# Attention head by head, or in groups of heads that fill a bank of 512 columns

## What is computed

```python
# mixer_a, layers 0 and 3: 16 heads of 64; tokens see chunks of 64 up to their own
s = einsum('bqhd,bkhd->bhqk', qc, kb) * scale + bias          # bias: a table by distance
p = softmax(where(valid, s, NEG_INF)); o = einsum('bhqk,bkhd->bqhd', p, vb)
# mixer_c, layer 2: 8 heads x 2 maps, bias -slope*|distance|
a = p[:, 0] - lam_full * p[:, 1];      o = einsum('bhqk,bkhe->bqhe', a, v)   # e = 128
# second model, twice each:
# nsa_attention: 8 heads, three branches (7 or 15 compressed keys, selected, window), sum by gates
# mla_attention: 4 heads, logits (qn.kn + qp.kp) * scale, causal
# memory_cross_attention: 4 heads of 128 over 256 memory tokens
```

## Time and profile before

| | |
|---|---|
| median of 3 runs | 3524.96 us |
| profiled execution | 3519.57 us, span 3517.8 us |
| TensorE busy | 3267.9 us (93%), 22679 matmul records |
| VectorE busy | 1888.6 us (54%) |
| ScalarE busy | 1490.2 us (42%) |
| GpSimd busy | 71.9 us (2%) |
| granted TensorE clock, mean | 0.948 of 2.4 GHz |
| DMA | 533.95 MB, mean 152 GB/s |

### The profile page before, as it was taken

How to read it: one execution, slowest core, us unless ns; L and a number is a source line. 1 busy time by engine, 2 the same in 40 slices (tenths; PEclk the granted TensorE clock), 3 DMA queues, 4 the chain that set the end, 5 groups by cost and what they waited for, 6 DMA issues and landing times.

```text
span 3517.8 us, 53612 instructions
## 1 busy us (share of the span) xinstructions
PE 3267.9 (93%) x22679; PEld 3041.3 (86%) x22679; DVE 1888.6 (54%) x2615; ACT 1490.2 (42%) x2303; POOL 71.9 (2%) x146
## 2 busy tenths in 40 slices
PE   8998999999999996999999999988789999888899
PEld 8987998988989895998988998986689999767897
DVE  5555555546545466545555554665555447555554
ACT  4444444444444443444444444334344443344443
POOL 0000000000000000000000000000000000000000
PEclk9999999999999998999998999986899998779999
DMA  6552555555555551454563456440235565213354
GB/s 222 193 186 83 163 188 165 182 178 162 185 169 191 182 173 37 163 192 161 189 200 97 138 181 190 150 145 13 96 125 166 189 180 162 86 40 104 126 176 143
DMA packets 434402, 533.95 MB, mean 152 GB/s; under 512 B 27330, under 2 KB 398452, under 8 KB 434164
## 3 DMA queue, kind: packets, MB, share of 16 engines
q1 hardware_dynamic: 421220, 512.22, 44.8%
q10 hardware_dynamic: 12944, 18.31, 1.7%
HBM read 528.33 MB, written 1.11 MB: 151 GB/s over the span
## 4 chain that ended last, share of the span: by engine, by line
PE 85%; DVE 7%; ACT 4%; issue 2%; DMA 1%; POOL 1%; SPq 1%; ACTq 0%; DVEq 0%; POOLq 0%
PE bank L633 84%; ACT sb_prT L1031 1%; DVE sb_sc L1559 1%; DVE sb_nmax L1561 1%; PE bank L794 1%; DVE sb_hT_low L1514 1%; DMA sb_slot<-in_w_in_dram 1%; POOL sb_rstd L1353 1%; ACT sb_prT L993 1%; DVE sb_low L1435 1%; ACT sb_pr L1094 0%; ACT sb_high L1020 0%; PE bank L671 0%; ACT sb_hT_high L993 0%; DVE sb_oT_low L1516 0%
## 5 line engine op out<-in xcount | busy, mean ns | idle before, releaser
L1435 DVE TENSOR_TENSOR sb_low<-sb_slot,sb_high 128x2048 fp32r<-128x2048 f32 (+1 forms) x480 | 1094.3, 2283 | 712.0 <-ACT sb_high L1020 711.4
L633 PE MATMUL bank<-sb_hT_high,sb_high 128*128 128x256 f32 x4264 | 1214.5, 285 | 22.1 <-DVE sb_hT_low L1514 16.3
L633 PE MATMUL bank<-sb_hT_low,sb_high 128*128 128x256 f32 x4264 | 1210.2, 284 | 0.0
L633 PE MATMUL bank<-sb_hT_high,sb_low 128*128 128x256 f32 x4264 | 1209.8, 284 | 0.0
L1020 ACT ACTIVATE sb_high<-sb_slot 128x2048 fp32r<-128x2048 f32 (+1 forms) x480 | 912.1, 1905 | 676.6 <-PE bank L633 589.9
L633 PEld LDWEIGHTS bank<-sb_hT_high,sb_high 128*128 128x128 f32 x4264 | 823.0, 193 | 26.6 <-DVE sb_hT_low L1514 17.5
L633 PEld LDWEIGHTS bank<-sb_hT_low,sb_high 128*128 128x128 f32 x4264 | 823.0, 193 | 0.0
L633 PEld LDWEIGHTS bank<-sb_hT_high,sb_low 128*128 128x128 f32 x4264 | 822.2, 193 | 0.0
L1071 ACT ACTIVATE sb_prT<-bank 128x256 f32<-128x256 f32 x220 | 84.3, 383 | 699.2 <-PE bank L633 699.2
L633 PE MATMUL bank<-sb_low,sb_hidden_high 128*128 128x512 f32 x880 | 350.8, 399 | 0.0
L633 PE MATMUL bank<-sb_high,sb_hidden_high 128*128 128x512 f32 x880 | 346.7, 394 | 0.0
(11 more groups left out here) (209 smaller groups left out, 3464.5 us busy)
## 6 DMA issues: line engine op xcount, KB each, us to landing
sb_slot<-in_ff_w_in_dram SPq DMA_DIRECT2D x176, 1024.0 KB, 5.2
sb_slot<-in_ff_w_out_dram SPq DMA_DIRECT2D x88, 1024.0 KB, 5.0
sb_slot<-in_w_gate_up_dram SPq DMA_DIRECT2D x44, 1024.0 KB, 5.2
sb_slot<-in_w_in_dram SPq DMA_DIRECT2D x42, 1024.0 KB, 5.3
sb_slot<-in_a_w_qkv_dram SPq DMA_DIRECT2D x24, 1024.0 KB, 5.2
sb_slot<-in_w_down_dram SPq DMA_DIRECT2D x22, 1024.0 KB, 5.0
sb_slot<-in_c_w_qkv_dram SPq DMA_DIRECT2D x12, 1024.0 KB, 5.2
sb_slot<-in_a_w_o_dram SPq DMA_DIRECT2D x8, 1024.0 KB, 5.2
```

Of the source, the lines that this page charges most:

```text
L633: return nc.tensor.matmul(o, lhsT, rhs, start=start, stop=stop)
L1435: V.tensor_tensor(low[i][:, 0:size], slots[n % SLOTS][:, 0:size], high[i][:, 0:size].bitcast(F32), ALU.subtract) \
```

## The change

The heads of a stage are taken in groups: four where a head has at most 128 keys, two where it has 256, so that the scores of a group, and its turned blocks, fill at most one bank of 512 columns. `groups_of` makes the groups out of the units; each turn of the three engines is now a group.

- VectorE does one scale-and-bias operation for the group with a three-dimensional bias operand (heads x keys, reversed; for causal and cross stages one line repeated for each head; for the differential stage one operation for each pair of maps, so two at four heads), and one maximum that gives one column for each head.
- ScalarE does one exponential for each head as before, but writes it over the scores in `sc`; `pr` is gone.
- One copy moves the turned blocks of the whole group. ScalarE does it for groups of 256 keys and now ahead of the exponentials of group i; VectorE does it for all others, behind the maximum of group i.
- VectorE waits for the transposes of group i-3, not its exponentials, before it writes `sc`.
- `sc` and `prT` have buffers of 512 columns, `nmax` four columns a buffer; `arena` is 512 columns shorter; `silu`, `hid_f`, `junk` and `diag` are views of the same buffers at other places.

```diff
-        sc = sb("sc", [P, 3, S])
-        nmax = sb("nmax", [P, 3])
-        pr = sb("pr", [P, 3, S])
-        prT = sb("prT", [P, 2, S])
+        sc = sb("sc", [P, 3, 2 * S])
+        nmax = sb("nmax", [P, 3, 4])
+        prT = sb("prT", [P, 2, 2 * S])
...
+        def groups_of(st):
+            kind, i = st
+            groups, units = [], units_of(st)
+            while units:
+                u = units[0]
+                n = 4 if u["kn"] <= P else 2
+                mine, units = units[:n], units[n:]
...
+                groups.append(dict(units=mine, n=n, t=u["t"], kn=kn, bias=bias, scale=scale,
+                                   rows=u["blocks"][0][1], blocks=len(u["blocks"]), width=P * n * len(u["blocks"]),
+                                   first=u["first"], last=mine[-1]["last"], acc=u["acc"],
+                                   copier="act" if kn == S else "dve"))
...
             def attention(st):
+                        for j, u in enumerate(g["units"]):
+                            for n, (q, k) in enumerate(u["qk"]):
+                                ins = mm(bank[:, j * g["kn"]:(j + 1) * g["kn"]], q, k, n == 0, n == len(u["qk"]) - 1)
                         ins.then_inc(scored.sem, scored.next((st, i)))
...
-                        pe.wait_ge(act_read.sem, act_read.at((st, "p", i - 3)))
+                        turned_by = act_read if g["copier"] == "act" else dve_read
+                        pe.wait_ge(turned_by.sem, turned_by.at((st, "p", i - 3)))
...
             def attention(st):
+                    if i >= 2 and groups[i - 2]["copier"] == "act":
+                        g = groups[i - 2]
                         act.wait_ge(transposed.sem, transposed.at((st, "p", i - 2)))
...
+                        copy(prT[0:g["rows"], i % 2, 0:g["width"]], TB.of((st, "p", i - 2))[0:g["rows"], 0:g["width"]]) \
                             .then_inc(act_read.sem, act_read.next((st, "p", i - 2)))
+                    if i < len(groups):
+                        g = groups[i]
+                        act.wait_ge(maxed.sem, maxed.at((st, i)))
+                        for j, u in enumerate(g["units"]):
+                            part_of = sc[:, i % 3, j * g["kn"]:(j + 1) * g["kn"]]
+                            ins = nc.scalar.activation(part_of, part_of, ACT.Exp, bias=nmax[:, i % 3, j:j + 1],
+                                                       accum_out=sums[:, u["t"], u["col"]:u["col"] + 1])
+                        ins.then_inc(weighed.sem, weighed.next((st, i)))
...
             def attention(st, evacuate):
-                            dve.wait_ge(weighed.sem, weighed.at((st, i - 3)))
+                            dve.wait_ge(transposed.sem, transposed.at((st, "p", i - 3)))
+                        for b, bias in enumerate(g["bias"]):
+                            cols = slice(b * bias.shape[1] * g["kn"], (b + 1) * bias.shape[1] * g["kn"])
...
+                            ins = V.scalar_tensor_tensor(o, s, g["scale"], bias, ALU.mult, ALU.add)
+                        settle(dve, ins, dve_read, (st, "s", i))
+                        V.tensor_reduce(nmax[:, i % 3, 0:g["n"]], sc[:, i % 3, 0:size].rearrange("p (h k) -> p h k", h=g["n"]),
+                                        AX.X, ALU.max, negate=True).then_inc(maxed.sem, maxed.next((st, i)))
+                    if 2 <= i <= len(groups) + 1 and groups[i - 2]["copier"] == "dve":
+                        g = groups[i - 2]
+                        dve.wait_ge(transposed.sem, transposed.at((st, "p", i - 2)))
...
+                        V.tensor_copy(prT[0:g["rows"], i % 2, 0:g["width"]], TB.of((st, "p", i - 2))[0:g["rows"], 0:g["width"]]) \
+                            .then_inc(dve_read.sem, dve_read.next((st, "p", i - 2)))
```

More of the change, by code:

```diff
@@ L795, in attention @@
                         ins.then_inc(transposed.sem, transposed.next((st, "p", i - 2)))
                     if i >= 3:
-                        u = units[i - 3]
-                        if u["first"]:
-                            banks[u["acc"]] = SUMMED.take(pe, u["acc"])
-                        pe.wait_ge(act_read.sem, act_read.at((st, "p", i - 3)))
-                        for b, (k0, n) in enumerate(u["blocks"]):
-                            ins = mm(banks[u["acc"]][:, u["c0"]:u["c0"] + u["width"]], prT[0:n, (i - 3) % 2, b * P:(b + 1) * P],
-                                     u["v"][b], b == 0, b == len(u["blocks"]) - 1)
+                        g = groups[i - 3]
@@ new lines, in attention @@
+                        if g["first"]:
+                            banks[g["acc"]] = SUMMED.take(pe, g["acc"])
+                        turned_by = act_read if g["copier"] == "act" else dve_read
+                        pe.wait_ge(turned_by.sem, turned_by.at((st, "p", i - 3)))
+                        for j, u in enumerate(g["units"]):
+                            for b, (k0, n) in enumerate(u["blocks"]):
+                                c = (j * g["blocks"] + b) * P
+                                ins = mm(banks[u["acc"]][:, u["c0"]:u["c0"] + u["width"]], prT[0:n, (i - 3) % 2, c:c + P],
+                                         u["v"][b], b == 0, b == len(u["blocks"]) - 1)
@@ L1549, in attention @@
             def attention(st, evacuate):
-                units = units_of(st)
-                for i in range(len(units) + 4):
-                    if i < len(units):
-                        u = units[i]
-                        kn = u["kn"]
+                groups = groups_of(st)
+                for i in range(len(groups) + 4):
+                    if i < len(groups):
+                        g = groups[i]
+                        size = g["n"] * g["kn"]
                         dve.wait_ge(scored.sem, scored.at((st, i)))
@@ L1565, in attention @@
+                    if i >= 4 and groups[i - 4]["last"]:
+                        g = groups[i - 4]
                         dve.wait_ge(matmul_done.sem, matmul_done.at((st, "pv", i - 4)))
-                        evacuate(u["acc"], G.of(u["acc"]))
+                        evacuate(g["acc"], G.of(g["acc"]))
             def heads(bank, n):
```

100 lines of the change are left out of this document (46 added, 54 removed).

## The result

The changed kernel takes 3390.17 us (median of 4 runs, 3386.27 to 3391.95) against 3523.27 us (median of 4, 3521.4 to 3529.39) for the kernel before on the same chip: a ratio of 0.9618, 95% interval 0.9601 to 0.9634. That is 133 us saved where 63 were forecast, outside the range on the fast side. The profiled execution took 3391.95 us (span 3390.2), 127.6 us of span less than before.

The account below looks back on a forecast made before the run. The prediction took a latency loop in attention, no engine's load, as the bound. Gains of 12.5 + 14.7 (chunked), 8.0 (differential), 19.0 (sparse) and 8.4 (latent, cross) summed to 62.6 us, giving 3462 us, range 3430 to 3494.

Parts of the forecast that it names:

- What bounds the kernel: Attention stages: a latency loop through ScalarE's order, 0.8 us of idle TensorE per turn of two 256-key heads.
- I therefore leave it there, at no gain.: Sparse stages: the clock stays at 1.2 GHz through the first 55 us, with no gain counted for it.
- the 9.5 us of waiting: Each sparse stage: forecast gain from less TensorE idling and evacuation hold-up, less a longer start; 19.0 us over two.
- clock regained: Rival, sparse stages: gapless runs of four heads bring 2.4 GHz back early, 20 us more each, 3422 us; chance 0.13.
- Chunked stages: Two sixteen-head stages: 17.6 us for 256-key groups, 10.6 for 128-key, start 2.5, sum 32.2 each; gains 12.5 and 14.7.
- The 1.48 us a group: VectorE's price for a group: bias 0.69, maximum 0.69 and 0.1 between.
- Exponentials: ScalarE, one for each head: 0.63 us each at 256 columns and 0.52 at 128, accumulator read included.
- Differential stage: VectorE bounds: 16.2 plus 19.3 us, start and end 4.5, making 40.0; gain 8.0.
- Latent and cross attention: Four short stages, mostly start and end: latent 11.6 us for 13.7, cross 11.4 for 13.5; gain 8.4 in all.
- VectorE or the handshakes: Rival, 82 groups: slower 512-wide operations or wider-spaced exponentials lose 31 of the 63 us, 3494 us; chance 0.2.
- no difference: Rival: time saved in attention is lost to the weights behind it, 3525 us; chance 0.02.
- slower: Rival: long silences at the nine stages' starts drop the clock to each stage's end, 59 us more, 3584; chance 0.03.

Follow-up runs that it names:

- single_new: Changed kernel with groups of one head everywhere and all copies of turned blocks on ScalarE, new order kept: ratio 0.9762 to the kernel before.
- single_old: Changed kernel with groups of one head, ScalarE's old order (exponentials before the copy) and all copies on ScalarE: ratio 0.9963 to the kernel before.
- wide_single: Changed kernel with the sparse stages' 128- and 256-key heads issued singly, 7- and 15-key heads still in fours: ratio 0.9703 to the kernel before.
- narrow_single: Changed kernel with only the sparse stages' 7- and 15-key heads issued singly, all others grouped: ratio 0.975 to the kernel before.
- narrow_last: single_new with the 7- or 15-key heads moved behind the 128- or 256-key ones in each half of a sparse stage: ratio 0.974 to the kernel before.
- allact: Changed kernel with the turned-block copies of four-head groups on ScalarE too: ratio 0.9575 to the kernel before.
- mix_act: Changed kernel with four-head groups' copies moved to ScalarE in chunked and differential stages alone: ratio 0.9594 to the kernel before.

## Why the prediction was wrong

**What bounds the kernel** was right: a loop in ScalarE's order, no engine's load. The new order alone saves 2.0% (single_new against single_old), and the 256-key part of a chunked stage runs at 2.20 us a group as worked out.

**The failing step: "I therefore leave it there, at no gain."** The sparse stages were priced at the lower clock for 55 us of each; the clock came back after 3.4. By the forecast's own rows 51.4 us of TensorE work at 1.2 GHz is 25.7 at 2.4, 51 us over two stages, and the miss there is 50.5 (69.5 against 19.0). That the two agree so closely is partly luck: TensorE's busy time in fact fell by 28.3 and 28.6 us, while the 9.5 us of waiting that the forecast saved in each stage was some 3 too much. The argument was the row itself: 94% busy, and still low. But that busy share was read as one thing, where the change alters what fills it: the shape and the order of the blocks. wide_single and narrow_single show that the level follows these. Nor was the row all that the record had. The forecast said that the chunked stages ran the same 128-key heads mostly at full clock; in the second one they ran at 0.50 from 1893.7 to 1905.0 (10.33 of 11.30 us busy), so the trace of the kernel before already had the same heads at both levels. The rival "clock regained" had the mechanism, a chance of 0.13, and a price of 20 us a stage, 5 short of what it gave; but it put the effect down to gapless runs of four heads, and narrow_single shows that grouping the wide heads does not bring it about while the narrow ones are issued alone (47.8 us down). Whoever had followed it would have been at 3422, with the rest of the miss in the steps below.

The Trainium skill ("TensorE: Matmul & The Clock Gate", section "What's actually happening") has it that activity releases the throttle. The changed kernel agrees, back at 2.4 GHz after 3.4 us. narrow_single does not, as long as activity is read as the busy time of the profile: 10.20 of 10.20 us busy at 0.50; nor does single_new, with 9.40 of 9.40. The forecast set this rule against one row and took the row; the row holds for the kernel before, the rule for the changed one.

**Chunked stages, 28.6 for 32.2.** The 256-key part is the 17.6 us of the forecast. The 128-key part was priced at VectorE's 2.65 us a group, and the start's 2.5 put on top. The stretch shows VectorE at 21.1 of 28.6 us: it has slack behind, in the 256-key groups, and scores run far enough ahead to lend it, so an engine that is slower in one part of a pipelined stage doesn't bound that part. TensorE's only long wait is the start (1.4 us). The 0.60 us for a 128-key head at full clock was near: in narrow_last one takes 0.56 (2350.71 to 2351.27). The 1.48 us a group was 1.33 in the trace: the reduction starts 0.72 behind the bias operation and the next bias operation 0.61 behind the reduction, before that has ended.

**Exponentials** stand 0.51 and 0.38 us apart for the forecast's 0.63 and 0.52. The accumulator's read begins before its exponential ends (298.48 against 298.57), and the next exponential begins before the read ends, so the read costs nothing beside the exponential's own time. That shortens each start, 4.3 us to the first transposes for 4.6.

**Differential stage, 33.3 for 40.0.** VectorE bounds it, as said: 29.98 of 33.3 us busy. The sum of its groups was right in kind, but 4.5 us of start and end were added although VectorE works through most of both, and each group was 0.15 or more too dear (a four-head group with its copy 2.03, from 1309.27 to 1311.30, for 2.2).

**Latent and cross attention, 10.9 and 10.5 for 11.6 and 11.4:** the same spacing of exponentials.

**What held:** the copy on VectorE in four-head groups is hidden in the chunked stages, where moving it to ScalarE (allact, mix_act) changes the stage by 0.1 us; in the differential stage, which VectorE bounds, it costs 1 us. VectorE did not become the bound elsewhere, no bias operation or maximum was dearer than 0.69, and the long silences at the starts cost no clock in the chunked stages (1.00). The rivals "VectorE or the handshakes", "no difference" and "slower" all fell. Small slips of the forecast (340 us of stages for 341, VectorE's least share 46% for 44%, 4.8 for 4.6 us in the 256-key heads of a sparse stage) move nothing. The 5.5 us between the median's 133.1 and the profile's 127.6 is the spread of single runs.

What brings the clock back is open. The runs vary it by the order and size of the blocks only; a stage with its narrow heads made 128 columns wide would separate width from blocks, and one without narrow heads would show what wide groups do by themselves; neither was tried.

## What to carry to other kernels

A stretch at the lower clock is not a constant of the kernel: when a change alters the size or order of TensorE's blocks there, price the clock both ways and give the faster one a real chance, even if the row says 94% busy. Here it paid to group the heads by kind, the narrow ones too: one narrow branch left in singles gave back nearly two fifths of the change (0.975 against 0.960). And where a stage is pipelined, compare each engine's sum over the whole stage, not only over its busiest part.

## What was not expected of the hardware

A TensorE without gaps can stay at 1.2 GHz (10.2 us in narrow_single, with lone 15-key heads among four-head groups; 9.4 us with 128-key heads alone in single_new), and one that waits can keep 2.4 GHz (kernel before, first chunked stage, 310.0 to 332.5: 18.14 of 22.50 us busy at 1.00). Lone narrow heads are dear: a 7-key head handed out alone takes 1.37 us at the lower level (2341.04 to 2342.41 in single_new), more than a 128-key head's 1.06, though it has a fraction of the columns. The accumulator's read of 0.19 us is hidden between exponentials that follow each other.
